# Eight pairs of tiles through seven products in the first half of both down projections, and the residual loaded later

## What is computed

```python
def swiglu(h, w_gate, w_up, w_down):
    return (jax.nn.silu(h @ w_gate) * (h @ w_up)) @ w_down

x = x + 0.5 * swiglu(rmsnorm(x, norm_ffn1[l]), w1_gate[l], w1_up[l], w1_down[l])
...  # mixer: projection, attention, pooling, output projection
x = x + 0.5 * swiglu(rmsnorm(x, norm_ffn2[l]), w2_gate[l], w2_up[l], w2_down[l])
return rmsnorm(x, norm_final)
```

## Time and profile before

| | |
|---|---|
| median of 3 runs | 1687.75 us |
| the profiled execution | 1687.65 us |
| its span, first to last instruction | 1685.8 us |
| TensorE, busy share of the span | 99% |
| VectorE | 86% |
| ScalarE | 55% |
| GpSimd | 14% |
| granted clock of TensorE, mean | 0.999 |

### The profile page before, as it was taken

How to read it: one execution, slowest core, us unless ns; L and a number is a source line. 1 busy time by engine, 2 the same in 40 slices (tenths; PEclk the granted TensorE clock), 3 DMA queues, 4 the chain that set the end, 5 groups by cost and what they waited for, 6 DMA issues and landing times.

```text
span 1685.8 us, 21945 instructions
## 1 busy us (share of the span) xinstructions
PE 1674.9 (99%) x7500; PEld 1389.3 (82%) x7500; DVE 1457.2 (86%) x1753; ACT 921.7 (55%) x1094; POOL 233.6 (14%) x397
## 2 busy tenths in 40 slices
PE   9999999999999999999999999999999999999998
PEld 7788888888888888888888888888888888888886
DVE  7999999999988787587977889999999999888896
ACT  6655555555555544454555545555555555555554
POOL 0222222222220000000040002222222222200000
PEclk9999999999999999999999999999999999999999
DMA  7677777777775655666544575777777777765564
GB/s 277 205 230 232 230 225 224 224 224 225 223 266 195 250 199 196 208 202 199 175 149 153 189 256 169 226 230 224 229 227 232 215 244 225 249 237 190 184 200 174
DMA packets 189502, 362.96 MB, mean 215 GB/s; under 512 B 12233, under 2 KB 24449, under 8 KB 189057
## 3 DMA queue, kind: packets, MB, share of 16 engines
q1 hardware_dynamic: 170528, 336.70, 59.3%
q0 software_dynamic: 16976, 24.14, 6.5%
q10 hardware_dynamic: 1936, 1.32, 0.3%
HBM read 346.39 MB, written 4.19 MB: 208 GB/s over the span
## 4 chain that ended last, share of the span: by engine, by line
PE 98%; DVE 1%; ACT 0%; issue 0%; DMA 0%; SPq 0%; ACTq 0%; DVEq 0%
PE banks L636 23%; PE banks L634 23%; PE banks L635 23%; PE banks L727 7%; PE banks L728 7%; PE banks L729 7%; PE banks L620 2%; PE banks L653 1%; PE banks L623 1%; PE banks L874 0%; PE banks L898 0%; DMA raw<-in_w_gate 0%; PE banks L886 0%; DVE w_lo L1373 0%; ACT gu L1051 0%
## 5 line engine op out<-in xcount | busy, mean ns | idle before, releaser
L1149 ACT ACTIVATE w_hi<-raw 128x1024 fp32r<-128x1024 f32 (+1 forms) x440 | 425.4, 997 | 288.9 <-PE banks L636 185.1
L1597 DVE TENSOR_TENSOR w_lo<-raw,w_hi 128x1024 fp32r<-128x1024 f32 (+1 forms) x440 | 491.4, 1144 | 52.6 <-ACT w_hi L1149 52.6
L634 PE MATMUL banks<-w_hi,act 128*128 128x512 f32 x1056 | 411.6, 390 | 0.0
L636 PE MATMUL banks<-w_lo,act 128*128 128x512 f32 x1056 | 410.9, 389 | 0.0
L635 PE MATMUL banks<-w_hi,act 128*128 128x512 f32 x1056 | 410.8, 389 | 0.0
L1187 ACT ACTIVATE w_hi<-raw 128x1024 fp32r<-128x1024 f32 x212 | 214.5, 1022 | 216.8 <-PE banks L636 170.9
L1692 DVE TENSOR_TENSOR w_lo<-raw,w_hi 128x1024 fp32r<-128x1024 f32 x212 | 246.5, 1177 | 75.6 <-ACT w_hi L1187 72.8
L634 PE MATMUL banks<-w_hi,h 128*128 128x512 f32 x688 | 267.8, 389 | 0.0
L636 PE MATMUL banks<-w_lo,h 128*128 128x512 f32 x688 | 267.7, 389 | 0.0
L635 PE MATMUL banks<-w_hi,h 128*128 128x512 f32 x688 | 267.6, 389 | 0.0
L2122 POOL DMA_DIRECT2D turned<-squared x320 | 170.9, 557 | 681.5 <-DVE squared L1448 675.7
(11 more groups left out here) (201 smaller groups left out, 1741.0 us busy)
## 6 DMA issues: line engine op xcount, KB each, us to landing
raw<-in_w_down SPq DMA_DIRECT2D x88, 1024.0 KB, 6.2
raw<-in_w_gate SPq DMA_DIRECT2D x84, 1024.0 KB, 5.2
raw<-in_w_up SPq DMA_DIRECT2D x84, 1024.0 KB, 5.4
raw<-in_w_in SPq DMA_DIRECT2D x32, 1024.0 KB, 5.4
raw<-in_w_out SPq DMA_DIRECT2D x16, 1024.0 KB, 5.0
turned<-squared POOLq DMA_DIRECT2D x320, 32.0 KB, 1.8
raw<-in_w_up POOLq DMA_DIRECT2D x20, 512.0 KB, 7.0
raw<-in_w_up SPq DMA_DIRECT2D x8, 512.0 KB, 9.4
```

What stands on the lines that cost most here:

```text
L634: pe.matmul(dst, operand[:, k, hi], w_hi[:, s, w], start=k == first, stop=False)
L636: mm = pe.matmul(dst, operand[:, k, hi], w_lo[:, s, w], start=False, stop=k == last)
L1149: act_e.activation(fast_split(w_hi, p, shift), fast_raw(name, shift), ACT.Copy).then_inc(hi_ready, 1)
L1597: dve.tensor_tensor(fast_split(w_lo, p, shift), fast_raw(ORDER[p], shift), fast_split(w_hi, p, shift).bitcast(F32), ALU.subtract).then_inc ...
```

## The change

Eight units in the first half of each down projection in place of six, with 1, 1, 2, 1, 1, 1, 1 and 2 plain chunks beside them; 60 pieces in place of 56. The chunks still are 22. A fourth stage of forms; the stages stand behind pieces 5, 16, 30 and 42 (before: 5, 20 and 36). The last tiles of h are rounded at piece 18 (before 16). The forms of eight units take all of `act` (32 KB in each partition), in four places, and stage 3 lies in the first. The raw forms lie at the start of `xr` instead of in `act`. So the residual can be loaded back only when all forms are made: its four loads of 512 KB go out together ahead of chunk 22, behind a wait for the fourth stage, instead of one each ahead of chunks 6 to 9. The second half of the second projection keeps its six units.

```diff
-UNITS = 6
-PAIR_CHUNKS = tuple((0, kc) for kc in range(3, 7)) \
-    + tuple(chunk for i in range(UNITS)
-            for chunk in (("unit", i), *(((0, 2 * i + 7), (0, 2 * i + 8)) if i < 2 else
-                                         ((1, 2 * i - 1), (1, 2 * i)))))
+UNITS, SECOND_UNITS = 8, 6
+BESIDE_UNIT = (1, 1, 2, 1, 1, 1, 1, 2)
+PAIR_ROWS = tuple((0, kc) for kc in range(8, 11)) + tuple((1, kc) for kc in range(4, 11))
+UNIT_CHUNK = tuple(4 + i + sum(BESIDE_UNIT[:i]) for i in range(UNITS))
+PAIR_CHUNKS = tuple((0, kc) for kc in range(4, 8)) \
+    + tuple(chunk for i, n in enumerate(BESIDE_UNIT)
+            for chunk in (("unit", i), *PAIR_ROWS[sum(BESIDE_UNIT[:i]):sum(BESIDE_UNIT[:i + 1])]))
...
 PAIR_PARTS = halves_of(range(4)) \
-    + tuple((c + dc, part) for c in range(4, 4 + 3 * UNITS, 3)
-            for dc, part in UNIT_PARTS + ((2, 0), (2, 1)))
+    + tuple((c + dc, part) for c, n in zip(UNIT_CHUNK, BESIDE_UNIT)
+            for dc, part in UNIT_PARTS + ((2, 0), (2, 1)) * (n - 1))
...
-PAIR_PIECES = 8 + 8 * UNITS
-SECOND_LAST = PAIR_PIECES + 8 + 6 * UNITS
-ROW_FORMS_AT = (5, 20, 36)
-ROW_LAST_H_AT = 16
-ROW_P1_AT = (54, SECOND_LAST - 2)
+PAIR_PIECES = len(PAIR_PARTS)
+SECOND_LAST = PAIR_PIECES + 8 + 6 * SECOND_UNITS
+ROW_FORMS_AT = (5, 16, 30, 42)
+ROW_LAST_H_AT = 18
+ROW_P1_AT = (PAIR_PIECES - 2, SECOND_LAST - 2)
...
-RESTORE_AT = (6, 7, 8, 9)
+RESTORE_AT, RESTORES = 22, 4
...
-        row_forms = at("row_forms", [P, 2, 4, UNITS, P], F32R, act_at + 4 * 2 * S * 4)
-        raw_row_forms = at("raw_row_forms", [P, 4, 2, P], F32, act_at + 2 * 2 * S * 4)
+        row_forms = at("row_forms", [P, 4, 2, 4, 2, P], F32R, act_at)
+        raw_row_forms = at("raw_row_forms", [P, 4, 2, P], F32, fast_at)
...
+        def row_forms_of(stage):
+
+            return row_forms[:, (stage + 1) % 4, :, :, :, :]
...
-                    if c in RESTORE_AT:
-                        if c == RESTORE_AT[0]:
-                            sp.wait_ge(product_ready, f["sb"] + GATE_SBS)
-                        n = RESTORE_AT.index(c)
-                        cols = slice(n * QCOLS, (n + 1) * QCOLS)
-                        sp.dma_start(xr[:, :, cols], (x_saved if f["turn"] else x)[:, cols]
-                                     .rearrange("(t p) n -> p t n", p=P)).then_inc(x_restored, 16)
+                    if c == RESTORE_AT:
+                        sp.wait_ge(product_ready, f["sb"] + GATE_SBS)
+                        sp.wait_ge(row_forms_ready, len(ROW_FORMS_AT) * (net(f) + 1))
+                        for n in range(RESTORES):
+                            held = slice(n * QCOLS, (n + 1) * QCOLS)
+                            sp.dma_start(xr[:, :, held], (x_saved if f["turn"] else x)[:, held]
+                                         .rearrange("(t p) n -> p t n", p=P)).then_inc(x_restored, 16)
...
-                begin = (12, (FT, 12)[t])[nb % 2] if pair else 0
+                k0 = 2 * (UNITS if nb < 2 else SECOND_UNITS)
+                begin = (k0, (FT, k0)[t])[nb % 2] if pair else 0
...
-                            dve.wait_ge(x_restored, (net(f) + 1) * 16 * len(RESTORE_AT))
+                            dve.wait_ge(x_restored, (net(f) + 1) * 16 * RESTORES)
```

More of the change, by code:

```diff
@@ L77 @@
 GATE_PIECES = (GATE_SBS - FAST_SBS) * 2 * SB_PIECES + FAST_SBS * FAST_PIECES
-UNITS = 6
-PAIR_CHUNKS = tuple((0, kc) for kc in range(3, 7)) \
-    + tuple(chunk for i in range(UNITS)
-            for chunk in (("unit", i), *(((0, 2 * i + 7), (0, 2 * i + 8)) if i < 2 else
-                                         ((1, 2 * i - 1), (1, 2 * i)))))
+UNITS, SECOND_UNITS = 8, 6
[5 more added lines that the diff above has]
+            for chunk in (("unit", i), *PAIR_ROWS[sum(BESIDE_UNIT[:i]):sum(BESIDE_UNIT[:i + 1])]))
 ROW_CHUNKS = tuple((nb, kc) for nb in (2, 3) for kc in range(FT // 4))
 SECOND_CHUNKS = tuple((2, kc) for kc in range(3, 7)) \
-    + tuple(chunk for i in range(UNITS)
+    + tuple(chunk for i in range(SECOND_UNITS)
             for chunk in (("second", i), (2, i + 7) if i < 4 else (3, i - 1))) \
@@ L96 @@
 PAIR_PARTS = halves_of(range(4)) \
-    + tuple((c + dc, part) for c in range(4, 4 + 3 * UNITS, 3)
-            for dc, part in UNIT_PARTS + ((2, 0), (2, 1)))
+    + tuple((c + dc, part) for c, n in zip(UNIT_CHUNK, BESIDE_UNIT)
+            for dc, part in UNIT_PARTS + ((2, 0), (2, 1)) * (n - 1))
 ROW_PARTS = halves_of(range(22, 44))
 SECOND_PARTS = halves_of(range(22, 26)) \
-    + tuple((c + dc, part) for c in range(26, 26 + 2 * UNITS, 2) for dc, part in UNIT_PARTS) \
-    + halves_of(range(26 + 2 * UNITS, 44))
+    + tuple((c + dc, part) for c in range(26, 26 + 2 * SECOND_UNITS, 2) for dc, part in UNIT_PARTS) \
+    + halves_of(range(26 + 2 * SECOND_UNITS, 44))
 DOWN_CHUNKS = (PAIR_CHUNKS + ROW_CHUNKS, PAIR_CHUNKS + SECOND_CHUNKS)
@@ L809, in row_form_product, with unit_piece @@
             def row_form_product(slot, j, form, i, bank, first, last):
[L811 to L816, removed]
+                hi, lo = (row_forms_of(i // 2)[:, part, form, i % 2, :] for part in range(2))
+                return add_product(bank, hi, lo, slot, j, first, last)
+            def unit_piece(part, i, slot, units):
+                begins, ends = i == 0, i == units - 1
                 if part == "F0":
@@ L854, in down @@
                     if is_unit(nb):
-                        unit_piece(part, kc, p % SPLIT_SLOTS).then_inc(piece_used, 1)
+                        unit_piece(part, kc, p % SPLIT_SLOTS,
+                                   UNITS if nb == "unit" else SECOND_UNITS).then_inc(piece_used, 1)
                     elif f["turn"] == 0 or p < count - TAIL_PIECES:
@@ L1192, in round_row_forms @@
                 act_e.wait_ge(raw_row_forms_ready, len(ROW_FORMS_AT) * net(f) + n + 1)
-                act_e.activation(row_forms[:, 0, :, 2 * n:2 * n + 2, :], raw_row_forms[:, :, :, :],
+                act_e.activation(row_forms_of(n)[:, 0, :, :, :], raw_row_forms[:, :, :, :],
                                  ACT.Copy).then_inc(row_forms_hi_ready, 1)
             def copy_row_p1(f, first, second):
-                last = (1 + 3 * UNITS, 24 + 2 * UNITS)[second]
+                last = (UNIT_CHUNK[-1], 24 + 2 * SECOND_UNITS)[second]
                 act_e.wait_ge(piece_used, first + DOWN_PIECES[net(f)].index((last, "F0")) + 1)
@@ L1730, in split_row_forms @@
                 dve.wait_ge(raw_row_forms_ready, done + 1)
[L1731 to L1732 removed]
+                dve.tensor_tensor(row_forms_of(n)[:, 1, :, :, :], raw_row_forms[:, :, :, :],
+                                  row_forms_of(n)[:, 0, :, :, :].bitcast(F32),
                                   ALU.subtract).then_inc(row_forms_ready, 1)
```

## The result

The changed kernel takes 1703.2 us (median of three runs, 1703.14 to 1705.65) against 1687.75: ratio 1.0095, 95% interval 1.0072 to 1.0118. It is slower by 15.4 us; 1702.1 had been forecast.

A forecast was written before the change was run, and what follows sets the result against it. TensorE was taken to bound the kernel, with VectorE to watch. Per projection, 8.5 us of stalls less 1.36 saved gave +7.2, so 1687.75 + 14.4 = 1702.1 us, range 1698 to 1707 (chance 0.72).

The forecast's parts named there:

- The savings: First half of each down projection: 6 of 510 matmuls go, 1.36 us less, 2.72 us for both projections.
- VectorE's short cycles: Cycles of 45 matmuls leave VectorE 0.53 us idle; a stage of forms costs 2.97 + 1.14, so 3.6 us short.
- The sum: VectorE's work per first half: two units and a fourth stage add 13.5 us to 98.0, giving 111.5 in 114.3 us.
- The eight gaps: TensorE stalls before pieces 17, 18, 20, 21, 35, 43, 44 and 47, 8.5 us per projection.
- ScalarE's wait for the forms: Sign in the first halves of the down projections: this wait lengthens; no size given.
- VectorE's wait for ScalarE: Sign in the first halves of the down projections: this wait falls from 15 us to a few.
- TensorE's start 0.13 us behind a late split: Delay read at one late split in the down projections; with 0.05 instead, the stalls are 8.3 us per projection.
- upper bound: Stalls of 9.3 us per projection if loads land 1 us later than 4.9 us, since piece 29 then starts late.
- The restores: Residual loads ahead of chunk 22: counted at nothing, 2.3 us to spare; late as a rival, 4.9 us per projection, chance 0.05.
- Not slower: Rival: VectorE's lead absorbs the stages in the first halves, no matmul waits, 1685.0 us; chance 0.07.
- Only the first of the moved stages hurts: Rival: only the stage at piece 16 stalls TensorE, 3.4 us per projection, 1694.6 us; chance 0.12.
- The clock: Rival: TensorE's granted clock falls below 1.00 in the first halves; chance 0.03.

The follow-up runs named there:

- e10: Changed kernel with each stage's work spread over the cycles and the long cycles fourth and eighth, same instructions: 1688.87 us, ratio 1.0006 to the kernel before.
- e1: Changed kernel with the additions that make the forms cut to 8 columns in stages 1, 2 and 3: 1693.46 us.
- e2: Changed kernel with three stages of forms moved from behind pieces 16, 30, 42 to behind 9, 27, 44, same instructions: 1690.33 us.
- e11: The changed kernel measured again, unaltered, as yardstick on the same chip as two other runs: 1703.89 us.
- e4: Changed kernel with the burst of residual loads halved, blocks 0 and 1 ahead of chunk 22, 2 and 3 ahead of chunk 26: 1704.25 us.
- e6: Changed kernel with only the second stage of forms moved, from behind piece 16 to behind piece 9: 1694.22 us.
- e3: Kernel before the change, with only the raw forms put in xr and the four residual loads together ahead of chunk 22: 1687.97 us.
- e5: Kernel before the change, with its two later stages of forms moved from behind pieces 20 and 36 to behind 18 and 34: 1690.13 us.
- e7: Changed kernel with the five additions of stages 1 to 3 moved to GpSimd, low parts left on VectorE: 1708.78 us.
- e8: Changed kernel with the additions and also the low parts of stages 1 to 3 moved to GpSimd: 1709.98 us.

## Why the prediction was right

**The savings.** 12 matmuls fewer, as counted. e10 shows the nearest to them alone, and even there the gaps take them back.

**VectorE's short cycles.** The sum had 13.5 us more work in a half. The trace has the 18 instructions more of the sum in the second projection (106 to 124) but 12.2 us more busy time (98.0 to 110.2); in the first it has 17 instructions and 11.0 us more (98.0 to 109.05). A part of what is missing is that instructions behind one another overlap (1.14 us from start to start where one takes 1.23); the rest wasn't followed up, and nothing in the forecast hung on this sum. The step that carried the forecast, a stage of 4.1 us in a cycle with 0.5 to spare, is shown by e1 (without the additions) and e2 (elsewhere). The eight gaps stand before the eight pieces named, each within 0.24 us of its size. Their sum without restarts is 8.0 us in the second projection, where 8.5 was forecast. ScalarE's wait for the forms grew as forecast, from 0.4 us in the first half of the first projection to 10.3.

Two of its readings were off. VectorE's wait for ScalarE was to fall from 15 us to a few; it fell only to 13.5 and 10.4 us, so that this sign of the mechanism did not come true. And TensorE's start 0.13 us behind a late split was no measured delay, since that matmul stands one pitch behind the one before it (1595.44). Where a split really was late it is 0.05 us before piece 17 (509.59 + 0.69 = 510.28 to 510.33), the lower of the two values that the prediction gives.

**What was left out of the sum.** The restart of 0.1 us behind each gap, 0.8 in a half; it makes up for gaps that came out 0.5 smaller in all, which is luck and not a term that was right. And the late load: in the first projection piece 29's chunk landed at 532.5 us; counted from the start of its half that is 1.9 us later than in the second projection.

```profile
532.53 2.01 ACT L1195 ACTIVATE w_hi<-raw 128x1024 fp32r<-128x1024 f32 x2 [3.57 <-DMA raw<-in_w_down]
```

ScalarE waits 3.57 us for it, VectorE comes late into the third stage, and piece 31 has the gap of 1.18 that in my steps "just fits". The prediction had such a load in its upper bound (9.3 in place of 8.5 us in a half, for loads 1 us later), but it came dearer: 1.18, 0.34 and two restarts, 1.7 us, in the first projection alone. It came again in e11 (0.54 and 0.33), e4 and e6. Why that load is slower than the other projection's was not tested. The forecast of 14.4 us is 1.0 under the 15.4 of the medians and 2.7 under the 17.1 of the two halves of the profiled execution, and this load is most of the second difference.

**The restores.** Counted at nothing, and nothing it was (e3, e4). The size of the margin was off: chunk 21 was issued at 577.5 and chunk 22 used at 592.6 us, 15.1 us later; I had 13.3, from the 375 GB/s of the earlier trace rows. In the second projection it was 13.9 us (1561.39 to 1575.32). The addition of block 0 ended at 594.84 + 1.28 = 596.1 us and TensorE took piece 60 at 596.6. So 0.5 us were to spare in the first projection and 1.6 in the second, not 2.3. By the 358 GB/s that the Trainium skill (DMA: Bandwidth & Descriptors, Specifications) gives, 4.19 MB take 11.7 us, 0.5 more than by my rate, and as an estimate worked out in my way the burst 13.8. The second projection agrees with that, the first is 1.3 us slower, so one figure does not give the landing of these six transfers.

**The rivals.** Not slower: the lead absorbed no stage but the first (the one on piece 5). Only the first of the moved stages hurts: no, those at 30 and 42 cost 1.0 and 2.8 us with their restarts, as e6 shows. The clock: 1.00 throughout the changed kernel, with gaps up to 1.7 us.

## What to carry to other kernels

Where a helper engine feeds the bound one through a small ring, the mean load of a stage says little: write down, piece by piece, when each is ready and when it is wanted, with durations from the trace; here the change lost some 18 us on a nearly full engine (the 15.4 lost and the 2.7 that the saved matmuls gave back), more than six times the saving. A burst of work on the helper is safer in front of large pieces than of small ones, above all where other extra work stands beside it (e5); moving three stages won back 13 of 16 us here. And before the bound engine's work is cut, ask what its helpers then have left: at 45 matmuls a cycle VectorE was nearly full, so the products saved could not be won in any order that was tried.

## What the hardware showed that I had not expected

**GpSimd beside VectorE.** Both on float32 additions in SBUF, VectorE's 512-column sum went from 0.69 to 1.10 us, or 2.76 beside GpSimd's 1024-column addition, which itself took 3.24 us. The rows of e7 above show why: the two take turns, instruction by instruction. GpSimd's addition ends at 547.17, 2.24 us after VectorE's split that was running when it began (544.93); VectorE's sum, begun at 544.96, ends at 547.72, 0.55 after GpSimd's addition; GpSimd's next ends at 548.30, 0.58 after that sum; VectorE's next at 548.86, 0.56 after that. A split that began beside such an addition took 3.39 us in place of 1.23:

```profile
511.45 3.22 POOL L2138 TENSOR_TENSOR gu<-h 128x1024 f32<-128x1024 f32 x1 [13.47 <-DVE row_forms L1740]
512.36 3.39 DVE L1701 TENSOR_TENSOR w_lo<-raw,w_hi 128x1024 fp32r<-128x1024 f32 x1
```

It ends 1.08 us after the addition, and beside all six of these additions in e7 VectorE's instruction ends 0.55 us (a sum) or 1.07 to 1.09 us (a split) behind them. Work moved to the idle engine lengthened the busy engine's work by more than it took off (111.7 us busy in a half of e7 against 109.2 in e11). The Trainium skill (SBUF — State Buffer, Who interferes with whom) has a rule for this: a VectorE instruction with two inputs in SBUF contends with a GpSimd instruction that reads SBUF, and the second to start waits for the whole of the first. The trace agrees with both parts.

**The clock after a gap.** In e7 TensorE ran at half pace for a while behind gaps of 2.2 and 3.0 us. The rows are stretches of e7 (columns as in the earlier trace rows) and TensorE by time:

```profile
512.00:516.00 4.00, 1.94 (x9) 1.32 (x8) 3.97 (x3) 0.00 (x0) 3.92 (x2) 1.00 0.99 382
517.00:524.00 7.00, 5.06 (x14) 3.51 (x13) 6.93 (x7) 2.52 (x3) 3.12 (x3) 0.53 0.04 15
```
```profile
515.81 0.50 PE L734 MATMUL banks<-w_hi,h 128*128 128x512 f32 x1 [2.06 <-DVE w_lo L1701]
...
516.61 0.44 PE L734 MATMUL banks<-w_hi,h 128*128 128x512 f32 x1
516.85 0.63 PE L735 MATMUL banks<-w_hi,h 128*128 128x512 f32 x1
517.27 0.63 PE L736 MATMUL banks<-w_lo,h 128*128 128x512 f32 x1
519.84 0.76 PE L641 MATMUL banks<-w_hi,h 128*128 128x512 f32 x1 [1.94 <-DVE w_lo L1701]
...
521.26 0.63 PE L641 MATMUL banks<-w_hi,h 128*128 128x512 f32 x1
521.68 0.63 PE L642 MATMUL banks<-w_hi,h 128*128 128x512 f32 x1
```

The granted clock is 0.53 in the second stretch, so about the lower of its two levels (1.2 of 2.4 GHz), and the pitch 0.427 us in place of 0.227. It had fallen before the second gap: the matmuls at 516.85 and 517.27 already are 0.42 us apart, four matmuls behind the one gap of 2.2 us. The same came behind the gap of 2.2 us in the second projection, behind the 3.0 us before piece 35 in both, and in e8 behind its 2.5 and 2.4 us before piece 35; it did not come in e8 behind 1.8 and 2.0 us, 1.3 us apart, nor in the changed kernel behind 1.65 and 1.18. Each time seven to ten matmuls ran so, which cost 1.6 to 2.4 us; in e7 7.8 us in all, beside 15.8 us of gaps. How much of the 7.8 would have come back as gaps at the full clock was not tested.

That is the fourth rival's mechanism, which the changed kernel, with gaps up to 1.65 us, didn't reach. The price put on it, 24 matmuls and 5.4 us a time, stood on no row and was more than twice too high. The rule of the Trainium skill (TensorE: Matmul & The Clock Gate, Why this matters for your kernels) against idle gaps between bursts of matmuls holds in e7 and e8.
